# Attention's k and probabilities turned in 32x32 blocks by VectorE, the blocks moved by GpSimd and SyncE, and the marks of a pair spread to unit 119

## The reference

```python
mq = rms_norm(to_heads(mq, MOBA_HEADS), q_norm_w)
mk = rms_norm(to_heads(mk, MOBA_HEADS), k_norm_w)
o_moba = moba_attention(mq, mk, to_heads(mv, MOBA_HEADS))
y_moba = from_heads(o_moba) * jax.nn.silu(mz)
...
y = jnp.concatenate([y_ret, y_gdn, y_moba], axis=-1)
return x + jnp.einsum('bte,ed->btd', y, w_out).astype(x.dtype)
```

## Time and profile before

| what | value |
|---|---|
| median of 3 runs | 510.7 us (510.6 to 510.95) |
| the profiled execution's own time | 510.59 us |
| its span, first to last instruction | 508.8 us |
| busy: TensorE, its weight loads, VectorE, ScalarE, GpSimd | 503.6, 424.1, 338.8, 279.0, 169.8 us |
| chain of work that ended last | 99% TensorE |
| GpSimd's block copies (L927) | 80 of `mT<-mT` and 56 of `kq<-mT` |
| loads of `w_out`: size, median to landing | 256 KB, 4.1 us |
| moves `kq<-mT` by SyncE: size, median to landing | 16 KB, 1.9 us |

### The profile page before, as it was taken

How to read it: one execution, slowest core, us unless ns; L and a number is a source line. 1 busy time by engine, 2 the same in 40 slices (tenths; PEclk the granted TensorE clock), 3 DMA queues, 4 the chain that set the end, 5 groups by cost and what they waited for, 6 DMA issues and landing times.

```text
span 508.8 us, 8943 instructions
## 1 busy us (share of the span) xinstructions
PE 503.6 (99%) x3442; PEld 424.1 (83%) x3442; DVE 338.8 (67%) x506; ACT 279.0 (55%) x464; POOL 169.8 (33%) x230
## 2 busy tenths in 40 slices
PE   8999999999999999999999999999999999999997
PEld 6888888888888888888888888888888888888885
DVE  5989998889766876564467455755567566646551
ACT  5776756764347676564537354664556456344340
POOL 5763245445122312134054115506050614230000
PEclk9999999999999999999999999999999999999999
DMA  8997666565654556473975676777775557757711
GB/s 280 346 323 200 166 162 169 159 174 144 190 132 122 132 158 158 134 197 69 292 196 145 167 222 164 201 196 190 193 187 168 166 172 232 221 185 222 260 43 41
DMA packets 154988, 92.61 MB, mean 182 GB/s; under 512 B 15971, under 2 KB 143938, under 8 KB 154946
## 3 DMA queue, kind: packets, MB, share of 16 engines
q1 hardware_dynamic: 151456, 89.86, 62.8%
q10 hardware_dynamic: 3490, 2.18, 1.5%
HBM read 89.00 MB, written 2.10 MB: 179 GB/s over the span
## 4 chain that ended last, share of the span: by engine, by line
PE 99%; POOL 0%; DVE 0%; DVEq 0%; issue 0%; POOLq 0%
PE pj L1574 20%; PE pj L1577 20%; PE pj L1576 20%; PE pj L1552 14%; PE pj L1553 7%; PE pj L1630 3%; PE pj L1639 2%; PE mx L1734 1%; PE pj L1549 1%; PE mx L1787 1%; PE mx L1769 1%; PE mx L1601 1%; PE pj L1647 1%; PE mx L1845 1%; PE mx L1907 1%; PE pj L1548 1%
## 5 line engine op out<-in xcount | busy, mean ns | idle before, releaser
L369 DVE TENSOR_TENSOR w_lo<-w_raw,w_hi 128x1024 fp32r<-128x1024 f32 x160 | 200.7, 1262 | 78.2 <-ACT w_hi L489 77.3
L489 ACT ACTIVATE w_hi<-w_raw 128x1024 fp32r<-128x1024 f32 x158 | 166.1, 1057 | 121.0 <-PE pj L1577 103.7
L1574 PE MATMUL pj<-w_hi,hT 128*128 128x512 f32 x320 | 126.5, 395 | 0.0
L1576 PE MATMUL pj<-w_hi,hT 128*128 128x512 f32 x320 | 126.1, 394 | 0.0
L1577 PE MATMUL pj<-w_lo,hT 128*128 128x512 f32 x320 | 124.7, 390 | 0.0
L1552 PE MATMUL pj<-hT,w_hi 128*128 128x512 f32 x300 | 109.0, 403 | 0.0
L1553 PE MATMUL pj<-hT,w_lo 128*128 128x256 f32 x300 | 84.1, 280 | 0.0
L1577 PEld LDWEIGHTS pj<-w_lo,hT 128*128 128x128 f32 x320 | 60.1, 188 | 12.2
L1574 PEld LDWEIGHTS pj<-w_hi,hT 128*128 128x128 f32 x320 | 60.1, 188 | 12.1
L1576 PEld LDWEIGHTS pj<-w_hi,hT 128*128 128x128 f32 x320 | 60.2, 188 | 11.5
L1552 PEld LDWEIGHTS pj<-hT,w_hi 128*128 128x128 f32 x300 | 56.3, 188 | 13.2 <-DVE w_lo L369 0.6
(11 more groups left out here) (239 smaller groups left out, 541.2 us busy)
## 6 DMA issues: line engine op xcount, KB each, us to landing
w_raw<-in_w_in_dram SPq DMA_DIRECT2D x256, 256.0 KB, 3.4
w_raw<-in_w_out_dram SPq DMA_DIRECT2D x64, 256.0 KB, 4.1
big<-in_x_dram SPq DMA_DIRECT2D x9, 256.0 KB, 5.3
out_dram<-sq ACTq DMA_DIRECT2D x7, 256.0 KB, 5.8
big<-in_x_dram SPq DMA_DIRECT2D x3, 512.0 KB, 7.1
cst<-table_dram SPq DMA_DIRECT2D x1, 682.0 KB, 9.3
kq<-vr SPq DMA_DIRECT2D x32, 16.0 KB, 1.8
kq<-mT SPq DMA_DIRECT2D x24, 16.0 KB, 1.9
```

The source lines that it names most:

```text
L369: eng.tensor_tensor(w_lo[:, n % NSPLIT, :], w_raw[:, n % NRAW, :], w_hi[:, n % NSPLIT, :].bitcast(F32), ALU.subtract).then_inc(S("lo"), 1)
L489: act.activation(w_hi[:, n % NSPLIT, :], w_raw[:, n % NRAW, :], ACT.Copy).then_inc(S("hi_done"), 1)
L1574: ins = pe.matmul(bank[:, :], src[:, kc, 0, tok], hi[:, k, :], start=first, stop=False)
L1576: pe.matmul(bank[:, :], src[:, kc, 1, tok], hi[:, k, :], start=False, stop=False)
```

## The change

The transposes of k and of the probabilities leave TensorE. Instead:

- VectorE multiplies k by its norm and by a row that holds the product of both norm weights and the scale (`qk_rows`, loaded in the opening by two more DMAs), in four instructions of 128 columns, and turns it in 32x32 blocks. It turns the probabilities likewise, 768 columns, into `big`.
- GpSimd moves half of the block groups of q, k and the probabilities (eight copies each), SyncE the other half (eight DMAs each). The output's sixteen groups are shared the same way. On SyncE these moves stand behind the loads of tiles 10, 12, 18 and 22 of the pair.
- The marks of a pair change: scores from 34 to 48, outputs from 62 to 91, the split of the outputs from 92 and 94 to 119 and 121. The turns of k and of the probabilities stand at 12 and 67.
- A pair's first head is evacuated 32 units later than before, since its buffer is read until mark 91 of the pair before (`EV_LATER`).
- One load of `x` for the residual moves from behind tile 143 to behind tile 151, since `big` holds the turned probabilities, and waits for their moves.

```diff
-U_MOBA = {"gate": 7, "ktr": 26, "score": 34, "pt": 54, "o": 62, "out": 72}
+U_MOBA = {"gate": 7, "k": 12, "score": 48, "p": 67, "o": 91, "out": 99}
+EV_LATER = 32
...
+        turned_k = aT[:, :, :]
+        keys_of = kq[:, 0].rearrange("p c k t -> p (c k) t")
+        turned_p = big[:, 6 * T:9 * T].rearrange("p (n t) -> p n t", n=6)
+        weights_of = kq[:, :].rearrange("p h c k t -> p (h c k t)")[:, 0:6 * P].rearrange("p (n t) -> p n t", n=6)
...
+            for parity, later in ((0, EV_LATER), (1, 0)):
+                g, rest = divmod(v - 1 - later, 64)
+                if GDN <= g < HEADS and g % 2 == parity and rest in (61, 63):
+                    return g, (rest - 61) // 2
+            return None
...
-                    sp.wait_ge(S("m_exp"), 4 * (MOBA // 2))
+                    sp.wait_ge(S("m_moved0"), 12 * (MOBA // 2))
+                    sp.wait_ge(S("m_moved1"), 16 * (32 * (MOBA // 2) - 8))
...
+            def spread_half(dst, src):
+
                 for d in (2, 3):
                     for q in range(4):
                         a, i = q * QUART, (q ^ d) * QUART
-                        sp.dma_start(queries_of[i:i + QUART, :, a:a + QUART], turned_q[a:a + QUART, :, i:i + QUART]).then_inc(S("m_q1"), 16)
-
-            SPREAD_Q_AT = {16 * (p + 1) + 10: (p, j) for p, (kind, j) in enumerate(PAIRS) if kind == "moba"}
+                        sp.dma_start(dst[i:i + QUART, :, a:a + QUART], src[a:a + QUART, :, i:i + QUART]).then_inc(S("m_moved1"), 16)
+
+            def spread_q(j):
+
+                sp.wait_ge(S("r_turned"), 2 * RET // 2 + 4 * j + 2)
+                spread_half(queries_of, turned_q)
+
+            def spread_k(j):
+
+                sp.wait_ge(S("r_turned"), 2 * RET // 2 + 4 * j + 3)
+                spread_half(keys_of, turned_k)
+
+            def spread_p(j):
+
+                sp.wait_ge(S("r_turned"), 2 * RET // 2 + 4 * j + 4)
+                spread_half(weights_of, turned_p)
+
+            def spread_out(p):
+
+                sp.wait_ge(S("y_turned"), p + 1 - FIRST_ROWS)
+                sp.wait_ge(S("yt_lo"), p - FIRST_ROWS)
+                spread_half(spread, turned)
+
+            MOBA_PAIRS = [(p, j) for p, (kind, j) in enumerate(PAIRS) if kind == "moba"]
+            SPREAD_OUT_AT = {16 * (p + 1) + 22: p for p, j in MOBA_PAIRS}
+            SPREAD_Q_AT, SPREAD_K_AT, SPREAD_P_AT = ({16 * (p + 1) + at: j for p, j in MOBA_PAIRS} for at in (10, 12, 18))
...
+                    sp.dma_start(qk_rows[:, 0, :], q_norm_w[0:1, :].broadcast_to([P, P])).then_inc(S("qk_in"), 16)
+                    sp.dma_start(qk_rows[:, 1, :], k_norm_w[0:1, :].broadcast_to([P, P])).then_inc(S("qk_in"), 16)
...
+                if p + 1 > FIRST_MOBA:
+                    act.wait_ge(S("m_moved1"), 16 * 32 * (p + 1 - FIRST_MOBA))
...
-                advance(U["ktr"] + 2)
-                act.wait_ge(S("m_ktr"), j + 1)
-                act.wait_ge(S("wqk"), 1)
-                act.activation(kT, mx[2][:, :], ACT.Copy, scale=sm[:, 23:24]).then_inc(S("m_kT"), 1)
...
-                move_blocks(spread, turned, "otr")
+                move_blocks(spread, turned, "otr", 4 if PAIRS[p][0] == "ret" else 2)
...
+                for i, (dst, src) in enumerate(((queries_of, turned_q), (keys_of, turned_k), (weights_of, turned_p))):
+                    pool.wait_ge(S("r_turned"), 2 * RET // 2 + 4 * j + 2 + i)
+                    move_blocks(dst, src, "m_moved0", 2)
+                    pool.wait_ge(S("m_moved0"), 12 * j + 4 * (i + 1))
...
+                advance(U["k"])
+                if j == 0:
+                    dve.wait_ge(S("qk_in"), 2 * 16)
+                    dve.scalar_tensor_tensor(qk_rows[:, 0, :], qk_rows[:, 0, :], SCALE, qk_rows[:, 1, :], ALU.mult, ALU.mult).then_inc(S("wqk"), 1)
+                    dve.wait_ge(S("wqk"), 1)
                 dve.wait_ge(S("m_pow"), j + 1)
-                rk = sm[:, 64:72].rearrange("p (n k) -> p n k", k=2)[:, :, 1:2].broadcast_to([P, 4, P])
-                dve.tensor_tensor(vT[:, :, :].rearrange("p h (c e) -> p (h c) e", c=C), both[:, :, 1, :], rk, ALU.mult).then_inc(S("kn"), 1)
+                for n in range(4):
+                    dve.scalar_tensor_tensor(vT[:, n // 2, n % 2 * P:(n % 2 + 1) * P], both[:, n, 1, :], sm[:, 65 + 2 * n:66 + 2 * n],
+                                             qk_rows[:, 0, :], ALU.mult, ALU.mult).then_inc(S("kn"), 1)
+                dve.wait_ge(S("kn"), 4 * (j + 1))
+                dve.transpose(turned_k.rearrange("p n t -> p (n t)"), vT[:, :, :].rearrange("p h t -> p (h t)")).then_inc(S("r_turned"), 1)
...
-                advance(U["pt"] + 2)
-                act.wait_ge(S("pt_psum"), 2 * j + 1)
-                act.activation(kT[:, 0:3 * P], mx[2][:, 0:3 * P], ACT.Copy).then_inc(S("pt_a"), 1)
...
+                advance(U["p"])
+                dve.transpose(turned_p.rearrange("p n t -> p (n t)"), th[:, 6 * P:12 * P]).then_inc(S("r_turned"), 1)
...
-                pe.wait_ge(S("kn"), j + 1)
-                for n in range(4):
-                    ins = pe.transpose(mx[2][:, n * P:(n + 1) * P], vT[:, n // 2, n % 2 * P:(n % 2 + 1) * P], ident)
-                ins.then_inc(S("m_ktr"), 1)
-                stream(U["score"])
-                pe.wait_ge(S("m_q0"), 4 * (j + 1))
-                pe.wait_ge(S("m_q1"), 16 * 8 * (j + 1))
-                pe.wait_ge(S("m_kT"), j + 1)
+                pe.wait_ge(S("m_moved0"), 12 * j + 8)
+                pe.wait_ge(S("m_moved1"), 16 * (32 * j + 16))
...
-                stream(U["pt"])
-
-                for h in range(2):
-                    pe.wait_ge(S("m_exp"), 4 * j + 2 * h + 2)
-                    for i in range(3):
-                        ins = pe.transpose(mx[(2, 0)[h]][:, i * P:(i + 1) * P], pr[:, h, i * P:(i + 1) * P], ident)
-                    ins.then_inc(S("pt_psum"), 1)
                 stream(U["o"])
-                pe.wait_ge(S("pt_a"), j + 1)
-                pe.wait_ge(S("pt_v"), j + 1)
+                pe.wait_ge(S("m_moved0"), 12 * j + 12)
+                pe.wait_ge(S("m_moved1"), 16 * (32 * j + 24))
```

More of the change, by code:

```diff
@@ L187, in layer @@
         sm = sb("sm", [P, 128 + 44 * GDN // 2])
+        qk_rows = sb("qk_rows", [P, 2, P])
         pj = [ctx.enter_context(nc.psum_tensor(f"pj{s}", [P, 512], F32)) for s in range(4)]
@@ L286, in layer @@
         FIRST_ROWS = GDN // 2
+        FIRST_MOBA = (GDN + RET) // 2
         turned = mT[:, 0:4, :]
@@ L352, in finished @@
             g, rest = divmod(v - 1, 64)
-            if v == 0 or g >= HEADS:
-                return None
-            if g == 0:
+            if v and g == 0:
                 return (0, (rest - 57) // 2) if rest >= 57 and rest % 2 else None
-            if g >= GDN:
-                return (g, (rest - 61) // 2) if rest in (61, 63) else None
-            return (g, rest // 16) if rest % 16 == 15 else None
+            if v and g < GDN:
+                return (g, rest // 16) if rest % 16 == 15 else None
+            for parity, later in ((0, EV_LATER), (1, 0)):
[3 more added lines that the diff above has]
+            return None
         def conv_at(h, i):
@@ L448, in spread_qk @@
                         sp.dma_start(head_qk(1)[i:i + QUART, :, a:a + QUART], turned_qk(1)[a:a + QUART, :, i:i + QUART]).then_inc(S("r_qk1"), 16)
-            def spread_q(p, j):
-                sp.wait_ge(S("r_turned"), 2 * RET // 2 + 2 * j + 2)
+            def spread_half(dst, src):
                 for d in (2, 3):
@@ L464, in _ @@
                 elif n in SPREAD_Q_AT:
-                    spread_q(*SPREAD_Q_AT[n])
+                    spread_q(SPREAD_Q_AT[n])
+                elif n in SPREAD_K_AT:
+                    spread_k(SPREAD_K_AT[n])
+                if n in SPREAD_P_AT:
+                    spread_p(SPREAD_P_AT[n])
+                if n in SPREAD_OUT_AT:
+                    spread_out(SPREAD_OUT_AT[n])
                 if n in (0, 1, 3, 5):
                     load_piece(sp, (n + 1) // 2 + 1)
-                for i in {11: (0, 1), 12: (2,), 15: (3,), 24: (4, 5), 26: (6, 7)}.get(n - HEADS * TPH, ()):
+                for i in {11: (0, 1), 12: (2,), 23: (3,), 24: (4, 5), 26: (6, 7)}.get(n - HEADS * TPH, ()):
                     load_x(i)
@@ L514, in evacuate @@
                 if p > (GDN + RET) // 2:
-                    act.wait_ge(S("kn"), p - (GDN + RET) // 2)
+                    act.wait_ge(S("kn"), 4 * (p - (GDN + RET) // 2))
                 act.activation(rows[g % 2][:, s].rearrange("p s e -> p (s e)"), pj[2 * (g % 2) + s][:, :], ACT.Copy,
@@ L1359, in turn_rows @@
                     dve.wait_ge(S("otr"), FIRST_ROWS + 4 * (p - FIRST_ROWS))
+                if p > FIRST_MOBA:
+                    dve.wait_ge(S("m_moved1"), 16 * 32 * (p - FIRST_MOBA))
                 dve.transpose(turned.rearrange("p n c -> p (n c)"), on[:, :, :, :].rearrange("p h c e -> p (h c e)")).then_inc(S("y_turned"), 1)
@@ L1890, in mix_moba @@
                 U = {k: base + v for k, v in U_MOBA.items()}
```

(15 more changed lines are left out.)

9 lines of the change are left out of this document (removed).

## The result

The changed kernel takes **514.59 us** (median of 7, 512.65 to 516.59) against 510.7 (510.42 to 511.1): ratio 1.0072, interval 1.0059 to 1.0084. The prediction was 511.0, with 514.3 as its upper end. Of the seven executions three have a mean granted clock of 1.000 (512.65, 512.99, 514.23 us) and four have 0.993 to 0.997 (514.59 to 516.59). The profiled one took 512.99 us, with a span of 511.0 at clock 1.000, so its trace shows the waits but not what the clock adds. The clock is not the whole spread either: the three at 1.000 lie 1.6 us apart, and executions of the kernel before lie up to 1.3 us apart without any stop.

The account below looks back on a forecast made before the run. TensorE's own list of products was taken as the bound, busy 503.6 of 508.8 us. The sum 510.6 - 3.3 + 3.35 + 3 x 0.1 + 3 x 0.05 = 511.1 gave a forecast of 511.0 us, range 509.3 to 514.3.

Parts of the forecast that it names:

- The transposes: On TensorE, ten transposes fewer in each of three pairs, 0.44 plus 0.66 us a pair: 3.3 us less.
- The stop at tile 142: TensorE waits once before output tile 142 for the last pair's yT: 3.3 to 3.4 us, summed as 3.35.
- The outputs: Output products at mark 91 wait for moved blocks of probabilities: 0.05 us a pair, three times.
- The bound of 0.96 a move: SyncE's 192-row moves of probabilities, issue time proportional to size: last lands at 447.9, 1.5 us late each time.
- The scores: Score products at mark 48 wait for moved blocks of q and k: 0.1 us a pair, three times.
- That the norms hold GpSimd: Beside VectorE's four k norms, GpSimd's copies are held as by w_lo; otherwise copies end at 428.9, no wait.
- rival C: The 3.3 us stop lets TensorE's clock fall to half speed: 1.5 us lost, 512.6 us; chance 0.10.
- B: Moved blocks come late at marks 48 or 91: 512 to 515.5 us, slower; chance 0.25.
- A: The time saved on transposes and the stop before tile 142 cancel: 510.2 to 511.7 us; chance 0.50.

Follow-up runs that it names:

- the kernel before with one number changed: The kernel before with mark out of the unit pairs at 96 in place of 72, nothing else changed: 515.64 us.
- The version without the stop: The changed kernel with the last two feature tiles of the output products reading pair 6's y in place of pair 7's: 509.9 us.
- k alone: Against the kernel before, k turned by blocks in all pairs, moves ahead of tile 12's load; probabilities by TensorE; y's moves two tiles earlier: 510.08 us.
- the last version: Changed kernel with k's moves earlier, pair 7's probabilities by TensorE, its y moves earlier, and pairs 5 and 6 at p 66, outputs 93, out 101: 508.31 us.

## Why the prediction was wrong

- **The transposes, -3.3.** Right, a little small: 3 x 1.13 = -3.4.
- **The stop at tile 142, +3.35.** Right in place, cause and size: 3.34, from the order of the instructions and the rows' own durations. The first products behind it stand further apart and add 0.09, so the stream is 3.43 us later.
- **The outputs, +0.15.** Right: 0. The turn took 0.97 us, the moves of 192 rows 0.606 each, 0.65 apart, and the last landed at 445.89 for products at 446.07. The bound of 0.96 a move was far off.
- **The scores, +0.3.** The mis-sized term: **1.93**. SyncE was the one late, not GpSimd, whose sixteenth copy ended at 428.35, 1.3 us ahead of the mark. The chain was named in the text: norms, turn, w_lo, the load that it releases, eight moves. Against TensorE's own time for the mark, pair 7's moves began 0.4 us later than predicted, and that is the norms: 1.49 us, where I took 1.1 from a like instruction in another stretch. The release adds 0.1 us behind the landing. Nothing was left to take this up, since the text put the landing level with the mark. Pairs 5 and 6 I took to be like pair 7; they lost 0.1 and 0.3 us more. In pair 6 that is the load ahead of the moves: 1.09 us of issue, where pair 7's took 0.80. That the norms hold GpSimd was wrong too: its copies beside them took 0.279 to 0.292, and the norms were slow themselves. The Trainium skill (GPSIMD Engine Reference, "Specifications") has GpSimd contend with VectorE instructions of two SBUF inputs; the traces agree for tensor_tensor (copies of 0.64 and 1.18 us in place of 0.28). For these scalar_tensor_tensor, which have two as well, they don't on GpSimd's side; whether the norms' own 0.41 to 0.46 us is that contention on VectorE's side no run here shows.
- **The clock, rival C at 0.10.** Its price, 1.5 us from the opening's products, is what was measured (1.46), in part by luck: the median mixes executions without a fall with others, and the three falls that were profiled cost 1.5, 1.7 and 2.9 us. The opening's rows show durations alone; the windows view has the granted clock at 1.00 there, so that this was the lower level was not shown. The chance was far too low. The Trainium skill (TensorE: Matmul & The Clock Gate, "Why this matters for your kernels") says that idling costs the higher clock, and the long stops bear it out in most executions, not in all: at 3.3 us four of seven runs of the changed kernel lost it, five of six with k's moves earlier, and five of six of the kernel before with one number changed; at 2.35 us two of twelve clearly did. That no row shows a fall was no evidence against it: before, there was no stop to show one.
- The cases were weighed as if one had to be true. B (1.93) and C (1.46) both came true on top of A, and the sum passes the range's end. So the steps that failed are the term of the scores (0.3 for 1.93) and the clock, which the sum had at nothing.

The sum with the measured terms: 510.7 - 3.4 + 3.43 + 1.93 + 1.46 = 514.1. **0.5 us stay open.** In the profiled executions, both at clock 1.000, the account is whole where the change acts: from tile 99 to the last product the changed kernel loses 1.96 us on the one before, and -3 x 1.13 + 1.93 + 3.43 is 1.97. The rest lies elsewhere. About 0.2 us is outside the span: an execution takes 1.89 to 2.09 us more than its span in the changed kernel and 1.74 to 1.85 in the one before; why isn't known. And 0.3 us came ahead of the attention pairs, between the first projection product (33.86, before 33.85) and tile 51. In the other profiles tile 51 starts from 0.1 us earlier to 0.7 us later than in that of the kernel before, in versions built on either kernel, so the traces give no sign that the change is the cause; that it has no part in it isn't shown. The version without the stop leaves 0.7 us (510.65 - 3.4 + 1.93 = 509.2, measured 509.9), k alone 0.6 (510.61 - 1.1 = 509.5, measured 510.08), and the last version 0.3 (510.75 - 2 x 1.19 - 0.36 = 508.0, measured 508.31); of each some 0.2 is outside the span as well.

## What to carry to other kernels

Where one engine bounds the kernel, work taken from it counts only if each new hand-over comes before its mark: follow every queue in which the new moves stand, up to the instruction that releases the load ahead of them. A stop of 3.3 us cost TensorE 1.46 us more than its length in the median, so price such a stop with the clock in it, and shorten or fill it. A route that is too long only for the last stage, where nothing follows to hide it, can be used for all stages but that one.

## What the runs showed of the hardware

- At a stop of about 3.3 us the clock fell in most executions, not in all of them (a mean of 0.997 or less in 15 of 20). In the three profiles that show it, it was at 0.50 for 3.4, 3.4 and 6.8 us. It fell 0.5 and 0.9 us before TensorE started again in two of them, and 1.3 us after in the third.
- Useless products in that stop gave 1.46 us back.
- A VectorE scalar_tensor_tensor with two SBUF tensors (128x128) left GpSimd's copies at 0.28 us and took 0.41 to 0.46 itself; a tensor_tensor of 128x512 held one to 0.64, and that of a w_lo (128x1024) one to 1.18 us.
- A move of 32 partitions by DMA takes 0.6 us of its queue whether 128 or 192 wide, and lands 1.8 to 4.7 us after its start, most often after 1.9 to 2.5.
